# The 24 gate columns of w_in in a two-layer decoder trunk: two passes on packed high and low parts in place of three passes on a full tile

## The chip, the cores and the metric

One core of one Trainium2 chip runs the whole kernel. The metric is device time in microseconds of one execution, the median over several; the kernel before has 3276.86 us (three runs, 3276.48 to 3279.43).

## The reference, cut to what matters

The reference is a trunk of two layers on 1024 tokens of width 1024, all in float32. Each layer normalises and modulates x, and projects it with w_in. The projection is cut into pieces: three of 512 columns for a gated convolution, 512 for the queries, six of 128 for keys and values, **24 columns of gate logits** (three branches times eight heads), and 2048 for two merge gates:

```python
z = h @ w_in[l] + b_in[l]
(cb, cc, cu, q, kc, vc, k_s, v_s, k_w, v_w, nsa_g, merge_g) = jnp.split(z, split_at, axis=-1)
...
g = jax.nn.sigmoid(gate_logits).reshape(B, S, 3, N_KV, HPG)[..., None]
o = g[:, :, 0] * o_cmp + g[:, :, 1] * o_sel + g[:, :, 2] * o_w
```

The 24 logits of a token, after a sigmoid, weight the three attention branches (compressed, selected, windowed) of its eight heads. After attention come an up projection, a merge, an output projection, and a squared-ReLU MLP.

## The kernel before, in words

**Products with two parts.** A float32 product on TensorE is made of parts rounded to fp32r, a form that streams one column per clock. Activations lie as hH (high part) and hL (what is left), with features on partitions and 1024 tokens along the free axis. Each weight tile is 128 output columns wide and has eight blocks of 128 rows (k = 0 to 7). GpSimd (POOL) splits it: the high part goes to `unit` (L1158), the rest to `wlo` (L1160), in two halves of four blocks. `dense` (L1163 to L1189) then makes, for each k, three passes of two halves of 512 tokens: high weights with hH, high weights with hL, low weights with hH. That is 48 matmuls for a tile, all summed in one of the two PSUM slots `lin0` and `lin1`, which chunks take in turn. A tile is loaded by SyncE as soon as its place in a ring of five raw slots is free. POOL splits a tile once the matmuls that read the high part two tiles earlier are done.

**Order around the change.** The order is written out by hand on every engine. TensorE does q3, ks, kw, ns (the 24 gate columns), vw, then small work, then vs, then the attention loop. The tile "ns" is loaded and multiplied like any other, 128 columns wide, of which 24 are used. ScalarE, after its part of the rotary work for kw (L1668), waits for the chunk ns and takes rows 0 to 23 of it through a sigmoid with bias (L1702) into rows 0 to 23 of `tmp[:, 1, :]`, which frees the PSUM slot; then it evicts vw (L1644, through `z`). TensorE, after vw, turns those 24 rows to token-major with eight transposes (L1362) into `aux`, each 24 rows by 128 tokens. Then it makes the compressed scores of the last query tile (L1369, plain float32), turns vw to token-major into the same `aux` (L1277), waits for all rotary work (`rope_made`), makes the first score (L1403 to L1409), and multiplies vs. VectorE ends its rotary work with the low part of kw (L1964), copies the gates from `aux` to `gates` in `tmp` (L2011), which gives `aux` free for vw's turn, clears a small tile (L2019), and goes on with the compressed scores (L2028).

**What else sets the order.** vw's turn on TensorE waits for the semaphore `aux_free`; the first score waits for `rope_made` of all seven rotated pieces; the attention loop waits for chunk vs and ScalarE's eviction of it. POOL makes constant tables at the start (`begin_gpsimd`, L776 to L828), among them `ident`, and reports them by `tab_made`. Lines that the prediction's steps touch besides: L1344 and L1352 (second matmul of the compression, 64 and 63 columns of weights), L1292 (its first matmul), L1422 (transposes of 63 columns), L1443 and L1444 (values).

Of the kernel before, what the change touches and what calls it, by code (L numbers as in the profile page):

```python
# [48 lines left out]
O_KC, O_VC, O_KS, O_VS, O_KW, O_VW = (O_Q + NH * HD + i * NKV * HD for i in range(6))  # L49
O_NSA = O_VW + NKV * HD  # L50
NG = 3 * NH
O_MG = O_NSA + NG
IN_W = O_MG + 2 * D

# [269 lines left out]
def trunk(nc, a, out):  # L324

    with ExitStack() as ctx:
        def sb(name, shape, dt=F32):
            return ctx.enter_context(nc.sbuf_tensor(name, shape, dt))
# [57 lines left out]
        ident = sb("ident", [P, P])  # L386
        identb = sb("identb", [P, P], BF16)
        ones = sb("ones", [P, P])
        sgn = sb("sgn", [P, 1])
        causal = sb("causal", [P, P], BF16)  # L390
        oldest = sb("oldest", [P, P], BF16)
# [384 lines left out]
        def begin_gpsimd(pool):  # L776
            n = [0]

            def then(ins):
                n[0] += 1  # L780
                ins.then_inc(pool_step, 1)
                pool.wait_ge(pool_step, n[0])
# [15 lines left out]
                then(ins)  # L798
            pool.sem_inc(tab_made, 1)

            then(pool.memset(identb[:, :], 0.0))
            keep(identb[:, :], ALU.not_equal, [[-1, P]], 0, 1, 1.0)
            for i in range(4):
# [199 lines left out]
        def layer_programs(layer):  # L1003
# [18 lines left out]
            def freed(eng, name):  # L1022

                c = CHUNK[layer, name]
                eng.wait_ge(lin_free[c % 2], c // 2 + 1)
# [68 lines left out]
            def gpsimd(pool):  # L1094
                def attention():


                    for u in range(len(STEPS)):
                        for st in SETS:
                            for i in range(HPG):  # L1100
                                if st["last"] + SCALED_AFTER[i] == u:
# [2 lines left out]
                                    pool.tensor_scalar(p, p, fac[:, st["no"] % 2, i:i + 1], 1.0, ALU.mult, ALU.mult).then_inc(p_scaled, 1)  # L1104
                                    pool.wait_ge(p_scaled, HPG * st["no"] + i + 1)

                def pair_forms(n):


                    p = KIND_NO[n]  # L1110
                    a11, a12, a21, a22 = (raw_block(n, j, kh) for j in range(2) for kh in range(2))
                    s1, s2, s4, s3 = (form_part(unitF, n, i, 1) for i in (1, 3, 5, 6))

                    def form_sum(i, x, y, op):
                        if FORM_PRIOR[n][i]:
                            released(pool, FORM_PRIOR[n][i])
                        pool.tensor_tensor(form_part(unitF, n, i, 1), x, y, op).then_inc(w_sum, 1)  # L1117

                    def form_low(i, x):
                        pool.wait_ge(form_hi, PRODUCTS * p + i + 1)  # L1120
                        pool.tensor_tensor(form_part(unit, n, i, 1), x, form_part(unit, n, i, 0).bitcast(F32), ALU.subtract).then_inc(form_lo, 1)  # L1121

                    pool.wait_ge(raw_in[SLOT[n]], IN_SLOT[n])
                    form_sum(1, a21, a22, ALU.add)
                    form_low(0, a11)
                    pool.wait_ge(w_sum, 4 * p + 1)
                    form_sum(3, s1, a11, ALU.subtract)
                    pool.wait_ge(w_sum, 4 * p + 2)
                    form_low(1, s1)
                    form_low(2, a12)  # L1130
                    form_sum(5, a12, s2, ALU.subtract)
                    pool.wait_ge(w_sum, 4 * p + 3)
                    form_low(3, s2)
                    form_low(4, a22)
                    form_sum(6, a11, a21, ALU.subtract)
                    pool.wait_ge(w_sum, 4 * p + 4)
                    form_low(5, s4)
                    form_low(6, s3)

                for n in [m for m in WEIGHTS if TILES[m][1] == layer]:  # L1140
# [13 lines left out]
                    for i, hf in enumerate(half):  # L1154
                        raw, high = wraw[:, SLOT[n], hf], unit[:, HI_AT[n][i], :]
                        if HI_PRIOR[n][i]:
                            released(pool, HI_PRIOR[n][i])
                        pool.tensor_scalar(high, raw, 1.0, 1.0, ALU.mult, ALU.mult).then_inc(w_hi, 1)  # L1158
                        pool.wait_ge(w_hi, 2 * s + i + 1)
                        pool.tensor_tensor(wlo[:, SLOT[n], hf], raw, high.bitcast(F32), ALU.subtract).then_inc(w_split, 1)  # L1160

            def tensor(pe):
                def dense(name, act_h, act_l, ready=None, beside=None, only=None, midway=None):  # L1163
# [9 lines left out]
                    for k in range(kk):  # L1173
# [4 lines left out]
                        for c, n, s, r, j in parts:  # L1178
# [8 lines left out]
                                    mm = pe.matmul(lin[c % 2][:, hf], w, m(k, hf), start=first, stop=last)  # L1187
                            if k == kk - 1:
                                mm.then_inc(lin_done, 1)  # L1189

                def first_pair():

# [161 lines left out]
                mm.then_inc(cmp_done, 1)  # L1354
                dense("ks", H, L)
                dense("kw", H, L)
                dense("ns", H, L)
                dense("vw", H, L)
                aux_begin("nsaT")
                freed(pe, "ns")  # L1360
                for t in range(NT):
                    mm = pe.transpose(aux[:, t * NG:(t + 1) * NG], tmp[0:NG, 1, t * P:(t + 1) * P], ident[0:NG, 0:NG])  # L1362
                mm.then_inc(aux_done, 1)

                def compressed_scores(bank, qt):
# [207 lines left out]
            def scalar(act):  # L1573
# [112 lines left out]
                for r in range(2):  # L1686
# [12 lines left out]
                rope_high("kw")  # L1699
                done(act, "ns")  # L1700
                act.wait_ge(rope_made, ROPED.index("ks") + 1)
                act.activation(tmp[0:NG, 1, :], slot("ns")[0:NG, :], ACT.Sigmoid, bias=cols[0:NG, R_NSA:R_NSA + 1]  # L1702
                               ).then_inc(free_sem("ns"), 1)
                z("vw", B(O_VW))
                act.wait_ge(rope_sum, len(ROPED))
                v_high("vw", vw, aux[:, :])

# [174 lines left out]
            def vector(dve):  # L1882
# [124 lines left out]
                rope("q3")  # L2007
                rope("ks")
                rope("kw")
                dve.wait_ge(aux_done, AUXED.index("nsaT") + 1)  # L2010
                dve.tensor_copy(gates[:, :, :].rearrange("p t n -> p (t n)"), aux[:, 0:NT * NG]).then_inc(aux_free, 1)  # L2011
                dve.wait_ge(rope_made, len(ROPED))
                dve.wait_ge(aux_free, AUXED.index("nsaT") + 1)

# [374 lines left out]
```

## Time and profile before

| | us |
|---|---|
| median of three runs | 3276.86 |
| lowest, highest | 3276.48, 3279.43 |
| profiled execution, its own time | 3278.76 |
| its span, first to last instruction | 3277.0 |
| TensorE busy | 3171.2 (97% of the span) |
| VectorE busy | 1855.7 (57%) |
| GpSimd busy | 1544.1 (47%) |
| ScalarE busy | 972.1 (30%) |
| TensorE clock granted, mean | 0.988 of full |

The profiled execution took 1.8 us more than its span, and 1.9 us more than the median. Busy times of TensorE come from matmuls whose ends are modelled, so two neighbouring matmuls overlap in it; the distance of their starts is what one costs. The stage of the change comes once in each layer, near 514 to 539 us and near 2127 to 2152 us.

### The profile page before, as it was taken

Reading aid. Unit: us, or ns where it says so; the run is one execution under the profiler, and the core shown is the slowest. Engines: PE = TensorE matmul, PEld = TensorE weight load, DVE = VectorE, ACT = ScalarE, POOL = GpSimd, SP = SyncE. Lnnn points to the kernel's source line nnn. Section 1 sums busy time; section 2 is a strip of 40 time slices with the busy share of each in tenths; the row PEclk is TensorE's granted clock in tenths of the full one; section 3 lists DMA queues with packets and bytes.
Section 4 is the critical chain, followed back from the end, with each engine's and each line's share of the span. In section 5 each row is a group of like instructions: output and inputs, shape, how many; then the busy total and the mean of one; then the engine's idle time right before and its main releaser. Section 6 shows DMA issues by size and latency. Waiting matters only on the chain.

```text
span 3277.0 us, 40421 instructions
## 1 busy us (share of the span) xinstructions
PE 3171.2 (97%) x15183; PEld 2589.9 (79%) x15213; DVE 1855.7 (57%) x2507; ACT 972.1 (30%) x1771; POOL 1544.1 (47%) x1727
## 2 busy tenths in 40 slices
PE   8999999998899999999999999999989999999998
PEld 6888887676688888888778888877767888888887
DVE  7533246887536666555565332478864545555555
ACT  2100114666212222222220001257661222222233
POOL 3433332233454656666744333323334656666665
PEclk8999999999899999999999999999999999999999
DMA  7333621000522222111243345200005211111112
GB/s 262 119 116 129 187 77 39 1 1 1 199 62 68 78 78 78 52 52 52 78 144 99 119 141 174 59 20 1 1 14 199 65 52 52 52 52 52 52 52 97
DMA packets 294440, 264.16 MB, mean 81 GB/s; under 512 B 10347, under 2 KB 274791, under 8 KB 293736
## 3 DMA queue, kind: packets, MB, share of 16 engines
q1 hardware_dynamic: 279410, 207.66, 21.2%
q10 hardware_dynamic: 14838, 53.94, 4.4%
q8 instruction: 122, 2.00, 0.3%
q14 instruction: 70, 0.57, 0.1%
HBM read 223.81 MB, written 30.41 MB: 78 GB/s over the span
## 4 chain that ended last, share of the span: by engine, by line
PE 87%; DVE 8%; issue 2%; ACT 2%; POOL 1%; DMA 0%; ACTq 0%; DVEq 0%; POOLq 0%; SPq 0%
PE lin L1187 56%; PE lin L1536 16%; PE aux L1427 2%; DVE pTL L2119 2%; PE pv L1443 2%; PE pv L1444 1%; DVE negm L2095 1%; PE lin L1403 1%; PE lin L1404 1%; PE pv L1292 1%; ACT pTH L1754 1%; PE lin L1369 1%; PE lin L1237 1%; PE lin L1238 1%; PE lin L1239 1%
## 5 line engine op out<-in xcount | busy, mean ns | idle before, releaser
L1158 POOL TENSOR_SCALAR unit<-wraw 128x512 fp32r<-128x512 f32 x396 | 324.9, 820 | 1002.4 <-PE lin L1187 687.0
L1187 PE MATMUL lin<-hH,unit 128*128 128x512 f32 x2272 | 715.0, 391 | 1.2 <-POOL wlo L1160 1.2
L1187 PE MATMUL lin<-hL,unit 128*128 128x512 f32 x2272 | 710.9, 389 | 0.0
L1187 PE MATMUL lin<-hH,wlo 128*128 128x512 f32 x2272 | 710.4, 389 | 0.0
L1160 POOL TENSOR_TENSOR wlo<-wraw,unit 128x512 fp32r<-128x512 f32 x396 | 562.6, 1421 | 33.0
L1187 PEld LDWEIGHTS lin<-hH,wlo 128*128 128x128 f32 x2272 | 426.5, 188 | 89.8
L1187 PEld LDWEIGHTS lin<-hL,unit 128*128 128x128 f32 x2272 | 426.5, 188 | 89.1 <-issue 0.2
L1187 PEld LDWEIGHTS lin<-hH,unit 128*128 128x128 f32 x2272 | 423.4, 188 | 88.8 <-issue 2.8
L1536 PE MATMUL lin<-fH,unit 128*128 128x512 f32 x1568 | 486.8, 390 | 4.2 <-DVE xT L2255 3.5
L2255 DVE SCALAR_TENSOR_TENSOR xT<-lin,adac,xT 128x512 f32<-128x512 f32 x448 | 328.9, 748 | 182.5 <-PE lin L1536 177.8
L1104 POOL TENSOR_SCALAR prob<-prob,fac 128x640 f32<-128x640 f32 (+7 forms) x256 | 184.2, 719 | 441.6 <-DVE fac L2089 423.7
L1536 PEld LDWEIGHTS lin<-fH,unit 128*128 128x128 f32 x1568 | 294.4, 188 | 67.0 <-issue 6.1
L1536 PE MATMUL lin<-fL,unit 128*128 128x512 f32 x784 | 305.0, 389 | 0.0
L2119 DVE TENSOR_TENSOR pTL<-aux,pTH 128x512 fp32r<-128x512 f32 (+8 forms) x296 | 198.4, 686 | 60.9 <-ACT pTH L1754 59.1
L1754 ACT ACTIVATE pTH<-aux 128x512 fp32r<-128x512 f32 (+8 forms) x296 | 173.4, 596 | 110.5 <-PE aux L1427 82.0
L2199 DVE TENSOR_TENSOR stage<-stage 128x1024 f32<-128x1024 f32 x32 | 46.1, 1440 | 280.2 <-ACT stage L1825 280.2
L568 DVE SCALAR_TENSOR_TENSOR adared<-wraw,cT,adared 128x256 f32<-128x256 f32 x280 | 194.8, 696 | 13.5 <-DMA wraw<-in_w_ada 4.1
L2095 DVE TENSOR_REDUCE negm<-lin 128x1 f32<-128x640 f32 (+7 forms) x256 | 177.7, 703 | 41.8 <-PE lin L1409 40.8
L1723 ACT ACTIVATE prob<-lin,negm 128x640 f32<-128x640 f32 (+7 forms) x256 | 178.7, 698 | 70.7 <-DVE negm L2095 69.4
L1427 PE MATMUL aux<-ident,prob 128*128 128x128 f32 x1056 | 162.0, 280 | 35.4 <-DVE pTL L2119 33.9
L1121 POOL TENSOR_TENSOR unit<-unitF,unit 128x256 fp32r<-128x256 f32 x224 | 179.4, 812 | 13.2
L1841 ACT ACTIVATE unit<-unitF 128x256 fp32r<-128x256 f32 x224 | 93.6, 418 | 308.2 <-POOL unitF L1117 308.2
(282 smaller groups left out, 4461.5 us busy)
## 6 DMA issues: line engine op xcount, KB each, us to landing
wraw<-in_w_ff SPq DMA_DIRECT2D x136, 512.0 KB, 3.9
wraw<-in_w_ada SPq DMA_DIRECT2D x80, 512.0 KB, 3.7
wraw<-in_w_in SPq DMA_DIRECT2D x78, 512.0 KB, 4.9
wraw<-in_w_o SPq DMA_DIRECT2D x24, 512.0 KB, 3.9
adar<-in_w_ada SPq DMA_DIRECT2D x16, 512.0 KB, 11.8
x_keep<-xT ACTq DMA_DIRECT2D x4, 2048.0 KB, 8.6
mix_keep<-tmp ACTq DMA_DIRECT2D x16, 512.0 KB, 3.1
gate_keep<-ropes ACTq DMA_DIRECT2D x16, 512.0 KB, 6.7
```

The lines of the kernel that those rows point to most:

```text
L568: ins = dve.scalar_tensor_tensor(out=total, in0=w[:, i, :], scalar=c, in1=total, op0=ALU.mult, op1=ALU.add)
L1104: pool.tensor_scalar(p, p, fac[:, st["no"] % 2, i:i + 1], 1.0, ALU.mult, ALU.mult).then_inc(p_scaled, 1)
L1121: pool.tensor_tensor(form_part(unit, n, i, 1), x, form_part(unit, n, i, 0).bitcast(F32), ALU.subtract).then_inc(form_lo, 1)
L1158: pool.tensor_scalar(high, raw, 1.0, 1.0, ALU.mult, ALU.mult).then_inc(w_hi, 1)
L1160: pool.tensor_tensor(wlo[:, SLOT[n], hf], raw, high.bitcast(F32), ALU.subtract).then_inc(w_split, 1)
L1187: mm = pe.matmul(lin[c % 2][:, hf], w, m(k, hf), start=first, stop=last)
L1427: mm = pe.transpose(o[:, i * P:(i + 1) * P], prob_of(no, i)[:, x["at"]:x["at"] + P], ident[:, :])
L1536: mm = pe.matmul(bank, w[:, k, :], m[:, i, k, :], start=BEGINS[i] and w is wh and m is fH and k == 0, stop=w is wl and k == 1, skip_group_ ...
L1754: act.activation(pt("high", x, r), turned(x, r), ACT.Copy).then_inc(t_hi, 1)
L2095: dve.tensor_reduce(negm[:, m:m + 1], scores(u)[:, at:at + st["n"]], AX.X, ALU.max, negate=True).then_inc(max_made, 1)
L2119: dve.tensor_tensor(pt("low", x, r), turned(x, r), pt("high", x, r).bitcast(F32), ALU.subtract).then_inc(t_free[x["bank"]], 1)
L2255: dve.scalar_tensor_tensor(out=xT[:, i, half[h]], in0=home[HOME[q][role]], scalar=adac[:, 5 * KC + i:5 * KC + i + 1], in1=xT[:, i, half[h] ...
```

## The change

The tile ns is still loaded 128 columns wide. POOL now splits only its first columns, and puts both parts into the place of the high part: columns 0 to 31 of each block hold the high part of the tile's columns 0 to 31, columns 32 to 55 hold the low part of columns 0 to 23. TensorE makes two passes for each k: 56 columns of weights with hH, which gives high times hH in rows 0 to 23 of the slot and low times hH in rows 32 to 55; then 24 columns with hL, added to rows 0 to 23. ScalarE evicts 56 rows with the bias and no sigmoid. The turn to token-major becomes a matmul with `fold`, a constant of two identity blocks one above the other (rows 0 to 23 and 32 to 55), which turns and adds the two row groups at once. The sigmoid is then done by ScalarE from `aux` straight to `gates`, after the eviction of vw, and VectorE's copy is gone; so ScalarE now frees `aux`. `fold` is made by POOL at the start.

```diff
@@ constants, tables
+NG_LO = 32
+        fold = sb("fold", [P, NG])
+            then(pool.tensor_tensor(fold[:, :], ident[:, 0:NG], ident[:, NG_LO:NG_LO + NG], ALU.add))
@@ gpsimd
+                def narrow_split(raw, high, made):
+                    raw, high = (x.rearrange("p (k n) -> p k n", n=P) for x in (raw, high))
+                    pool.tensor_scalar(high[:, :, 0:NG_LO], raw[:, :, 0:NG_LO], 1.0, 1.0, ALU.mult, ALU.mult).then_inc(w_hi, 1)
+                    pool.wait_ge(w_hi, made)
+                    pool.tensor_tensor(high[:, :, NG_LO:NG_LO + NG], raw[:, :, 0:NG], high[:, :, 0:NG].bitcast(F32),
+                                       ALU.subtract).then_inc(w_split, 1)
...
+                        if t[6] == ["ns"]:
+                            narrow_split(raw, high, 2 * s + i + 1)
+                            continue
@@ tensor
+                def narrow(name, act_h, act_l):
+                    c, n = CHUNK[layer, name], TILE_OF[layer, name]
+                    s, out = KIND_NO[n], lin[c % 2]
+                    pe.wait_ge(lin_free[c % 2], c // 2)
+                    for k in range(KC):
+                        if k % (KC // 2) == 0:
+                            pe.wait_ge(w_split, 2 * s + 2 * k // KC + 1)
+                        for hf in half:
+                            pe.matmul(out[0:NG_LO + NG, hf], high_of(n, k * P, NG_LO + NG), act_h(k, hf), start=k == 0,
+                                      stop=False, skip_group_check=True)
+                        for hf in half:
+                            mm = pe.matmul(out[0:NG, hf], high_of(n, k * P, NG), act_l(k, hf), start=False,
+                                           stop=k == KC - 1, skip_group_check=True)
+                    mm.then_inc(lin_done, 1)
...
-                dense("ns", H, L)
+                narrow("ns", H, L)
                 dense("vw", H, L)
                 aux_begin("nsaT")
+                pe.wait_ge(tab_made, 3)
                 freed(pe, "ns")
                 for t in range(NT):
-                    mm = pe.transpose(aux[:, t * NG:(t + 1) * NG], tmp[0:NG, 1, t * P:(t + 1) * P], ident[0:NG, 0:NG])
+                    mm = pe.matmul(aux[:, t * NG:(t + 1) * NG], tmp[0:NG_LO + NG, 1, t * P:(t + 1) * P], fold[0:NG_LO + NG, :],
+                                   start=t == 0, stop=t == NT - 1, skip_group_check=True)
@@ scalar
-                act.activation(tmp[0:NG, 1, :], slot("ns")[0:NG, :], ACT.Sigmoid, bias=cols[0:NG, R_NSA:R_NSA + 1]
-                               ).then_inc(free_sem("ns"), 1)
+                act.activation(tmp[0:NG_LO + NG, 1, :], slot("ns")[0:NG_LO + NG, :], ACT.Identity,
+                               bias=cols[0:NG_LO + NG, R_NSA:R_NSA + 1]).then_inc(free_sem("ns"), 1)
                 z("vw", B(O_VW))
+                act.wait_ge(aux_done, AUXED.index("nsaT") + 1)
+                act.activation(gates[:, :, :].rearrange("p t n -> p (t n)"), aux[:, 0:NT * NG], ACT.Sigmoid).then_inc(aux_free, 1)
@@ vector
-                dve.wait_ge(aux_done, AUXED.index("nsaT") + 1)
-                dve.tensor_copy(gates[:, :, :].rearrange("p t n -> p (t n)"), aux[:, 0:NT * NG]).then_inc(aux_free, 1)
```

## Rows read from the trace of the kernel before

**Rows 1.** The page: busy times, and the chain that ended last, by engine and by line.
```profile
PE 3171.2 (97%) x15183; PEld 2589.9 (79%) x15213; DVE 1855.7 (57%) x2507; ACT 972.1 (30%) x1771; POOL 1544.1 (47%) x1727
PE 87%; DVE 8%; issue 2%; ACT 2%; POOL 1%; DMA 0%; ACTq 0%; DVEq 0%; POOLq 0%; SPq 0%
```

**Rows 2.** The chain, 490 to 560 us, in order: start, us, what.
```profile
491.84 43.74 PE lin L1187 x192
535.59 0.60 PE aux L1362 x8
```

**Rows 3.** Timeline of PE around ns, both layers: start, us, engine, line, op, names, count.
```profile
513.66 0.39 PE L1187 MATMUL lin<-hH,unit 128*128 128x512 f32 x1
524.54 0.39 PE L1187 MATMUL lin<-hH,unit 128*128 128x512 f32 x1
535.52 0.67 PE L1362 MATMUL aux<-ident,tmp 24*128 24x24 f32 x8
536.12 2.00 PE L1369 MATMUL pv<-kcmp,qS 128*128 128x63 f32 x16
538.75 0.42 PE L1403 MATMUL lin<-kwH,qS 128*128 128x384 f32 x1
...
2148.38 0.67 PE L1362 MATMUL aux<-ident,tmp 24*128 24x24 f32 x8
```

**Rows 4.** Timelines of PE and its weight loads, weights going 128, 64, 63, 128 columns.
```profile
470.32 0.61 PE L1187 MATMUL lin<-hH,wlo 128*128 128x512 f32 x2
470.87 0.41 PEld L1344 LDWEIGHTS pv<-tmp,w 128*64 128x64 f32 x4 [0.35 <-issue]
471.03 0.49 PE L1344 MATMUL pv<-tmp,w 128*64 128x126 f32 x3
...
491.39 0.45 PE L1352 MATMUL pv<-w,tmp 128*63 128x64 f32 x5
491.77 0.50 PE L1187 MATMUL lin<-hH,unit 128*128 128x512 f32 x1
492.11 0.39 PE L1187 MATMUL lin<-hH,unit 128*128 128x512 f32 x1
```

**Rows 5.** Timeline of PE where form or kind changes without a stop.
```profile
452.51 0.39 PE L1187 MATMUL lin<-hH,wlo 128*128 128x512 f32 x1
452.74 7.30 PE L1292 MATMUL pv<-blk,cmp_k 128*128 128x126 f32 x64
...
558.74 0.22 PE L1409 MATMUL lin<-causal,identb 128*128 128x128 bf16 x1
558.80 0.27 PE L1422 MATMUL aux<-ident,tmp 128*63 128x128 f32 x1
```

**Rows 6.** Timelines of ACT and DVE, 526 to 541 us.
```profile
531.17 1.11 ACT L1702 ACTIVATE tmp<-lin,cols 24x1024 f32<-24x1024 f32 x1
535.69 1.11 ACT L1644 ACTIVATE fbuf<-lin,cols 128x1024 f32<-128x1024 f32 x1 [3.41 <-PE lin L1187]
531.25 4.92 DVE L1964 TENSOR_TENSOR kwL<-ropes,kwH 64x1024 fp32r<-64x1024 f32 x4 [4.45 <-ACT kwH L1668]
536.22 0.36 DVE L2011 COPY tmp<-aux 128x192 f32<-128x192 f32 x1
538.22 0.68 DVE L2028 TENSOR_TENSOR scm<-pv,cmask 128x504 f32<-128x504 f32 x1 [1.38 <-PE pv L1369]
```

**Rows 7.** Timelines of ACT: small activations, 8 and 512 elements a partition.
```profile
6.65 0.18 ACT L892 ACTIVATE csig<-pv 128x8 f32<-128x8 f32 x1
559.44 0.59 ACT L1754 ACTIVATE pTH<-aux 63x512 fp32r<-63x512 f32 x1 [0.51 <-PE aux L1422]
```

**Rows 8.** Timeline of POOL: start of the kernel, split of ns.
```profile
33.62 0.62 POOL L1158 TENSOR_SCALAR unit<-wraw 128x512 fp32r<-128x512 f32 x1 [16.99 <-DMA wraw<-in_w_in]
503.13 0.62 POOL L1158 TENSOR_SCALAR unit<-wraw 128x512 fp32r<-128x512 f32 x1 [7.75 <-PE lin L1187]
503.84 1.29 POOL L1160 TENSOR_TENSOR wlo<-wraw,unit 128x512 fp32r<-128x512 f32 x1
```

## The prediction, made before the change was run

> **What bounds the kernel now.** I read the page first. TensorE is busy for 97% of the span, and of the chain that ended last 87% is TensorE [rows 1]. So a change in a dense stage is worth what it takes from TensorE's own queue there, unless another wait ends later. The chain through the stage confirms it: 192 matmuls of L1187 in a row, the tiles ks, kw, ns and vw, and the eight transposes of the gates right behind them, with nothing of another engine between [rows 2]. The timeline gives prices. The tile ns starts at 513.66 and vw at 524.54: 10.88 us for 48 matmuls, 0.227 us each; the transposes take 0.60 us, from 535.52 to 536.12 [rows 3]. The second layer's transposes start 1612.9 us later and are as long [rows 3], so I work out one layer and double it.
>
> **Matmuls removed.** Of 48, 16 go: 16 x 0.227 = 3.63 us per layer, all on the path. The 32 left still stream 512 tokens each, and I take 0.227 us for the streaming: 7.25 us.
>
> **What the new weight widths add.** This is where I differ from that simple count. In `dense` every matmul has 128 columns of weights and each load runs beside the matmul before. The new tile goes from 56 to 24 columns and back for every k. The trace has two places where ordinary products change from 128 columns to 64 or 63, and in both the load is not ahead. The last product of 512 columns starts at 470.55 (two of them, 0.22 apart, from 470.32), and the load for L1344 begins only at 470.87 [rows 4]: 0.32 us instead of 0.227, so 0.09 us for the stop. Then the load itself is exposed: the first L1344 takes 0.16 us to the second (470.87 to 471.03), the later ones 0.11, so 0.053 us for 64 columns [rows 4]. On the way back, the last L1352 starts at 491.62 (five from 491.39, 0.057 apart), L1187 follows 0.15 later, again 0.09 over, and the next L1187 comes after 0.34 in place of 0.227: 0.11 us for 128 columns [rows 4]. Where the width stays 128 there is no stop, although the product changes from fp32r to plain float32: L1292 starts 0.23 after the L1187 before it [rows 5]. So the change of form is what costs, not the type. By columns the exposed load is about 0.83 ns each (estimate from the 64 and the 128): 0.047 us for 56 and 0.020 us for 24.
>
> No row shows a change between two narrow widths. From below it costs 0, as in the transposes of 63 columns, which follow a bf16 matmul of 128 columns after 0.06 us, with no stop at all [rows 5]. From above I take 0.14 us a change, half again over the 0.09. I choose 0.09, because the products of L1344 and L1352 are the nearest in kind, and transposes are the only ones without a stop. Then ns costs 7.25 + 16 x 0.09 + 8 x (0.047 + 0.020) = 9.23 us, and the way back to vw adds 0.09 + 0.11 = 0.20. Together 9.43 against 10.88: **1.45 us gained per layer**, not 3.63.
>
> The rows alone give that choice. The Trainium skill (TensorEngine Tiling (Array Packing), section Key Properties) states a rule that speaks against this change: a change of tiling mode, not of the tile alone, drains the TensorE, and it lists 64 and 32 columns as different modes. The trace agrees for 128 to 64, with the 0.09 us; for 64 to 32 no row here shows it. By that rule ns would come to the 9.23 us, without it to 7.39 us and the sum to that of the first rival below.
>
> **The turn.** Eight transposes go and eight plain float32 matmuls come, with 128 columns of weights (tokens) and 24 moving. A plain float32 product shows as two instructions: the eight heads of the compressed scores are 16, from 536.12, the whole 2.00 us long with a last one of 0.28, so about 0.112 us each once they run, and 0.05 more for the first load [rows 3]. That is with 63 moving columns; the time is that of the weights, since 126 moving columns also give 0.112 (64 of L1292 in 7.30 us) [rows 5]. So 15 distances of 0.112, 0.05 for the first load, and 0.15 from the last to the next product, as behind L1352 [rows 4]: 1.88 us against 0.60. **1.28 us lost per layer.** From below the bound is 0.60, as the transposes had; from above 2.0.
>
> **ScalarE and VectorE.** The gate eviction stays 1.11 us and reads 56 rows in place of 24. It waits behind kw's rotary work, starts at 531.17 as before and ends at 532.28 [rows 6]. vw on TensorE would end about 535.5 - 1.45 = 534.1, so this is not a wait. vw's eviction moves to 534.3 to 535.4. Then the sigmoid of 128x192 waits for the turn, which ends near 536.1; by activations of 8 and of 512 elements it takes between 0.18 and 0.59 us [rows 7], I take 0.35, and `aux` is free at 536.5. On TensorE stand behind this wait vw's turn, and behind that the first score; but the compressed scores, 1.8 us, come first and end near 538.0, so it costs nothing. If that cover were gone it would cost 0.4. VectorE loses the copy of 0.36; its clearing waits for ScalarE until 536.5, but it has nothing to do before 537.9, when the scores are there (it idled 1.38 for them before) [rows 6]. The last rotary product ends at 536.17 and the first score starts at 538.75, so 2.5 us is the most that this stage could move up before kw is the wait [rows 3, 6].
>
> **POOL.** Two splits of 0.62 + 1.29 us become a quarter of the elements or less, some 3 us less per layer. POOL begins ns at 503.13, when ks frees the place, and TensorE wants it at 513.66; POOL stands still for 7 us before it [rows 8]. Worth nothing. vs's split waits for ns to end and comes 1.6 us earlier; it has 10 us before it is used. `fold` is one more operation of 128x24 at the start, some 0.3 us, before a wait of 17 us for the first weights [rows 8]. SyncE's and the other queues' DMAs stay as they are.
>
> **Sum.** -1.45 + 1.28 = -0.17 us per layer, -0.3 us for two. The profiled execution of 3278.8 would become 3278.5, and the median, which lies 1.9 below it, 3276.6. The measurement can tell about 0.2%, 6.6 us, from no change.
>
> **Rivals.** (1) *No stop between the two narrow widths.* Only the entry and the way back stop: ns takes 7.25 + 0.14, the way back 0.20, so 3.29 us less, then 1.28 lost in the turn; the gate eviction, ended at 532.28, then cuts off 0.2. 1.8 us per layer, 3.7 in all: 3273.2. For it speaks L1422. (2) *The turn is cheap as well*: another 1.3 us per layer, until kw's rotary work cuts it at 2.5 per layer: 3271.9. Against it stand all plain float32 products in the trace. This is also what a tile with unchanged widths would come near to, if the narrow forms were not treated as such. (3) *Slower: narrow fp32r products stream at half the rate.* No fp32r product with fewer than 128 columns of weights is in the trace. Its place is the 32 matmuls of ns, its price 32 x 0.227 = 7.25 us per layer, so 3276.6 + 14.5 = 3291.1. It decides once a narrow matmul costs 0.10 us more than I say. Against it: L1344 with 64 columns has 0.11 for 126 moving columns, as L1292 has with 128 [rows 4, 5].
>
> **How the numbers follow.** My forecast 0.62; no stop between narrow widths 0.25; both cheap 0.02; half rate 0.05; something unseen of a few us, either way, 0.06. Nothing that I can name reaches 6.6 us of gain: faster 0.03, for the unseen. Slower gets half rate and its share: 0.08. The rest, 0.89, is within 0.2%. The range holds the stops from 0 to 0.14 us (3273.2 to 3278.0), the turn's bounds, and the 3 us that runs of one kernel differ by: 3272.0 to 3280.0.
>
> **What would show it.** At the new line, pairs of narrow matmuls with distances of 0.27 and 0.32, then 0.25 and 0.32 us; each first weight load of a pair behind the matmul before, put down to "issue". ns start to vw start 9.3 us (7.4 by the first rival, 16.5 by half rate). The turn: 16 instructions in 1.9 us. The compressed scores start near 536.1, and the first score near 538.6. The forecast is wrong if the score starts before 537.5 or after 540, or if TensorE waits for `aux`.

## The result, and the profile after

The changed kernel takes **3288.48 us** (median of 8, 3286.59 to 3289.87) against 3278.46 for the kernel before on the same chips (8 runs, 3276.27 to 3280.67): ratio 1.0028, 95% interval 1.0018 to 1.0038. It is slower, by some 10 us, where I had forecast 0.3 us less and a range that ended at 3280.0. Its profiled execution took 3289.87 us, 1.4 above its median, with a span of 3288.0.

The page of the changed kernel, busy times and the chain by engine; they answer to [rows 1]:

```profile
PE 3174.7 (97%) x15167; PEld 2588.8 (79%) x15197; DVE 1860.8 (57%) x2505; ACT 971.0 (30%) x1773; POOL 1539.1 (47%) x1728
PE 86%; DVE 9%; ACT 3%; issue 2%; POOL 0%; DMA 0%; ACTq 0%; DVEq 0%; POOLq 0%; SPq 0%
```

TensorE's share of the chain fell by one point, those of VectorE and ScalarE rose by one each: somewhere the end now hangs on them. And TensorE is busy 3.5 us longer although it has 16 fewer matmul instructions: some of them became slower.

The narrow tile itself isn't at fault. Timeline of TensorE in the changed kernel, from the last dense product before ns to the first after it:

```profile
515.43 0.61 PE L1202 MATMUL lin<-hH,wlo 128*128 128x512 f32 x2
515.89 0.63 PE L1216 MATMUL lin<-hH,unit 128*56 128x512 f32 x2
516.36 0.62 PE L1219 MATMUL lin<-hL,unit 128*24 128x512 f32 x2
...
522.86 0.63 PE L1219 MATMUL lin<-hL,unit 128*24 128x512 f32 x2
523.33 0.62 PE L1202 MATMUL lin<-hH,unit 128*128 128x512 f32 x2
```

The pairs start 0.46 or 0.47 apart, dense pairs 0.45: 32 products in 523.33 - 515.89 = 7.44 us, 0.232 each. So there is no stop on the way in, between 56 and 24 columns, or on the way out. The tile took 10.88 us before [rows 3].

The loss lies behind it. The chain of the changed kernel through this stage, in order of time (start, us, what):

```profile
525.48 2.13 DVE ropes L1979
527.61 1.56 DVE ropes L1982
...
529.19 2.21 DVE ropes L1987
...
535.75 1.12 ACT tmp L1736
...
537.00 3.58 PE aux L1395 x16
540.58 3.60 PE pv L1403 x16
544.18 1.71 PE aux L1309 x8
```

Before, this chain was TensorE's alone [rows 2]. Now it runs through kw's three rotary operations on VectorE, the copies of kw on ScalarE (left out here), ScalarE's eviction of the gates (L1736), and only then the turn. TensorE's own row for the turn names the wait, and the products behind it are twice as long as before:

```profile
537.00 3.58 PE L1395 MATMUL aux<-fold,tmp 56*128 56x24 f32 x16 [2.62 <-ACT tmp L1736]
540.51 3.67 PE L1403 MATMUL pv<-kcmp,qS 128*128 128x63 f32 x16
543.97 1.92 PE L1309 MATMUL aux<-ident,fbuf 128*128 128x128 f32 x8
545.54 0.67 PE L1437 MATMUL lin<-kwH,qS 128*128 128x384 f32 x1
...
2154.25 3.30 PE L1395 MATMUL aux<-fold,tmp 56*128 56x24 f32 x16 [2.62 <-ACT tmp L1736]
```

The compressed scores took 2.00 us before [rows 3] and take 3.67; the first products of the first score 0.42 and 0.67. Windows over the same stretch give the reason (window, us, then busy time and number of PE, PEld, DVE, ACT and POOL, then the granted clock, DMA share and GB/s):

```profile
515.90:523.30 7.40, 7.40 (x33) 3.72 (x32) 3.90 (x3) 4.41 (x5) 3.80 (x4) 1.00 0.23 52
534.00:537.00 3.00, 0.38 (x2) 0.03 (x1) 1.17 (x1) 2.95 (x4) 0.00 (x0) 0.94 0.48 141
537.00:540.50 3.50, 3.50 (x16) 3.45 (x16) 3.46 (x4) 0.86 (x1) 0.00 (x0) 0.50 0.08 29
540.50:544.00 3.50, 3.50 (x18) 3.50 (x18) 0.35 (x2) 0.33 (x1) 0.00 (x0) 0.50 0.00 0
544.00:547.00 3.00, 3.00 (x16) 2.65 (x15) 2.04 (x3) 1.02 (x1) 0.00 (x0) 0.52 0.00 0
547.00:550.00 3.00, 3.00 (x15) 2.49 (x15) 2.89 (x5) 1.92 (x3) 0.00 (x0) 1.00 0.00 0
```

The narrow tile ran at a granted clock of 1.00 (2.4 GHz). TensorE then stood still for 2.62 us, and the clock was 0.50 (1.2 GHz) for the ten microseconds of small products behind that. It had fallen shortly before the turn began (0.94 in the window 534 to 537). The second layer is alike, only that there it fell 0.3 us behind the start of the turn, whose first two distances are still 0.11 us and the later ones 0.21.

Why ScalarE is late is seen on POOL and VectorE. POOL of the changed kernel, the four operations for vs:

```profile
523.68 0.62 POOL L1173 TENSOR_SCALAR unit<-wraw 128x512 fp32r<-128x512 f32 x1 [3.48 <-PE lin L1219]
524.39 2.13 POOL L1175 TENSOR_TENSOR wlo<-wraw,unit 128x512 fp32r<-128x512 f32 x1
526.50 1.59 POOL L1173 TENSOR_SCALAR unit<-wraw 128x512 fp32r<-128x512 f32 x1
528.17 2.14 POOL L1175 TENSOR_TENSOR wlo<-wraw,unit 128x512 fp32r<-128x512 f32 x1
```

and VectorE beside it:

```profile
525.48 2.13 DVE L1979 TENSOR_TENSOR ropes<-fbuf,cosT 128x1024 f32<-128x1024 f32 x1
527.53 1.62 DVE L1982 TENSOR_TENSOR ropes<-rotated,sinT 128x1024 f32<-128x1024 f32 x1
529.19 2.20 DVE L1987 TENSOR_TENSOR ropes<-ropes 128x1024 f32<-128x1024 f32 x1
```

In the kernel before these three operations were:

```profile
522.88 1.23 DVE L1943 TENSOR_TENSOR ropes<-fbuf,cosT 128x1024 f32<-128x1024 f32 x1
524.02 1.22 DVE L1946 TENSOR_TENSOR ropes<-rotated,sinT 128x1024 f32<-128x1024 f32 x1
525.28 1.52 DVE L1951 TENSOR_TENSOR ropes<-ropes 128x1024 f32<-128x1024 f32 x1
```

and POOL's split of vs was:

```profile
524.89 0.83 POOL L1158 TENSOR_SCALAR unit<-wraw 128x512 fp32r<-128x512 f32 x1 [6.90 <-PE lin L1187]
525.80 2.14 POOL L1160 TENSOR_TENSOR wlo<-wraw,unit 128x512 fp32r<-128x512 f32 x1
...
528.62 1.29 POOL L1160 TENSOR_TENSOR wlo<-wraw,unit 128x512 fp32r<-128x512 f32 x1
```

POOL may start vs's split when ns is done on TensorE. Counted from the first instruction of the tile ks (491.77 before, 494.00 in the changed kernel), that now happens 3.4 us earlier, at 29.7 in place of 33.1. VectorE's work for kw does not move with it (31.5, before 31.1): the two that used to overlap for about one operation now overlap throughout. Both lose: VectorE's operations take 1.62 to 2.20 us, POOL's subtractions 2.13 and 2.14 and its second copy 1.59, where undisturbed ones take 1.29 and 0.62.

The stage can be laid out in microseconds from the start of the tile ks, layer 0 / layer 1. These are starts of the first instruction of each group, and the end of the last kwL operation; the last column is the first product of the next group of scores, behind the tile vs:

| kernel | ScalarE's gate eviction | kwL ends | turn | scores | vw's turn | first score | next score group |
|---|---|---|---|---|---|---|---|
| before | 39.40 / 39.38 | 44.39 / 44.38 | 43.75 / 43.75 | 44.35 / 44.35 | 46.18 / 46.18 | 46.98 / 46.98 | 60.30 / 60.30 |
| after | 41.75 / 41.75 | 46.75 / 46.75 | 43.01 / 43.01 | 46.51 / 46.24 | 49.98 / 49.70 | 51.54 / 51.27 | 65.47 / 65.62 |

So per layer: without the wait the turn would start at 40.32 (seen below), 3.43 us before the old 43.75. The wait takes back 2.69 (2.62 by its row, where the end before it is modelled); the turn costs 3.50 in place of 0.60, the scores 3.47 in place of 1.83, vw's turn 1.56 in place of 0.80, and the stretch up to the next score group 13.93 in place of 13.32: together 5.2 us lost in layer 0 and 5.3 in layer 1, 10.5 of the 11.0 by which the spans differ. The rest is made of pieces of both signs elsewhere (+2.2 us before the first tile ks, -2.5 and -1.1 in the two attention loops, +1.7 between the layers, +0.2 at the end), which also differ among the kernels below.

Much of the difference in the loops is the clock again. From the next score group to the last score of the loop the changed kernel takes 283.3 us in layer 0, with a granted clock of 0.50 for 2.4 us of it; the kernel before takes 285.7, with 10.2 us at 0.50, in its profiled execution. Among the profiled executions of all kernels here the loop takes 281.8 to 282.2 us in layer 0 with none of it at 0.50, 282.8 to 283.4 with 3.4 us at 0.50, and 284.7 with 6.8.

### The profile page after: what moved, and what is told of

It reads as the page before. It is cut to its first block, busy times and chain, and to the rows that moved or that the text cites. A ratio compares the mean times of both kernels' runs of the same rounds, so it can differ in the third digit from the quotient of the medians.

```text
span 3288.0 us, 40392 instructions
## 1 busy us (share of the span) xinstructions
PE 3174.7 (97%) x15167; PEld 2588.8 (79%) x15197; DVE 1860.8 (57%) x2505; ACT 971.0 (30%) x1773; POOL 1539.1 (47%) x1728
## 4 chain that ended last, share of the span: by engine, by line
PE 86%; DVE 9%; ACT 3%; issue 2%; POOL 0%; DMA 0%; ACTq 0%; DVEq 0%; POOLq 0%; SPq 0%
PE lin L1202 54%; PE lin L1570 16%; PE aux L1461 2%; DVE pTL L2153 2%; PE pv L1477 2%; PE pv L1478 1%; PE lin L1437 1%; DVE negm L2129 1%; PE lin L1438 1%; PE pv L1324 1%; ACT pTH L1790 1%; PE lin L1403 1%; PE lin L1269 1%; PE lin L1270 1%; PE lin L1271 1%
## 5 line engine op out<-in xcount | busy, mean ns | idle before, releaser
L1202 PE MATMUL lin<-hH,unit 128*128 128x512 f32 x2240 | 706.6, 392 | 1.5 <-POOL wlo L1175 1.5
L1202 PE MATMUL lin<-hL,unit 128*128 128x512 f32 x2240 | 701.5, 390 | 0.0
L1202 PE MATMUL lin<-hH,wlo 128*128 128x512 f32 x2240 | 700.9, 389 | 0.0
```

## The experiments

My theory after seeing this: POOL's earlier split slows kw's rotary work, the gate eviction, queued behind kw's copies on ScalarE, comes late, and TensorE's wait lets the clock fall. The rivals: the narrow tile or the plain products of the turn themselves bring the clock down, or the turn is the cost whatever else is done. Each experiment has runs of the kernel before beside it, with medians from 3277.81 to 3279.77, and the ratios are to these. The changed kernel was measured beside 3278.46, so a distance from it can be off by some 1.3 us. The layout of the stage, in the same measure, each row from one profiled execution (e7 has that of the kernel before within 0.01):

| kernel | gate eviction | kwL ends | turn | scores | vw's turn | first score | next score group |
|---|---|---|---|---|---|---|---|
| e1_evict_first | 31.48 / 31.48 | 46.75 / 46.75 | 40.32 / 40.32 | 42.21 / 42.21 | 45.30 / 44.04 | 46.86 / 46.81 | 61.38 / 60.14 |
| e2_split_late | 39.08 / 39.08 | 44.08 / 44.08 | 40.33 / 40.34 | 42.21 / 42.21 | 44.04 / 44.81 | 44.85 / 46.38 | 58.14 / 59.80 |
| e3_both | 31.09 / 31.09 | 44.08 / 44.08 | 40.32 / 40.32 | 42.21 / 42.21 | 44.04 / 44.04 | 44.84 / 44.84 | 58.14 / 58.16 |
| e4_full_width | 39.37 / 39.37 | 44.36 / 44.37 | 43.75 / 43.75 | 45.64 / 45.64 | 47.47 / 48.27 | 48.27 / 49.83 | 61.57 / 64.81 |
| e5_add_before_turn | 31.10 / 31.09 | 44.02 / 44.02 | 40.32 / 40.32 | 40.92 / 40.92 | 42.75 / 42.76 | 44.07 / 44.07 | 57.38 / 57.40 |
| e8_scores_first | 41.76 / 41.76 | 46.75 / 46.75 | 43.01 / 43.01 | 40.23 / 40.23 | 45.36 / 46.51 | 46.98 / 48.13 | 61.08 / 62.47 |
| e9_pool_beside | 41.68 / 41.66 | 46.67 / 46.66 | 43.75 / 43.75 | 44.35 / 44.35 | 47.12 / 47.10 | 47.97 / 47.95 | 61.29 / 61.26 |
| e10_gates_late | 39.37 / 39.37 | 44.37 / 44.37 | 46.23 / 46.23 | 46.83 / 47.20 | 48.66 / 50.67 | 50.19 / 52.24 | 64.40 / 66.05 |

(In e10 the eviction named is the first of six; the one that counts starts 5.7 us later.)

**Eviction of the gates ahead of kw's copies** (on the changed kernel):

```diff
@@ scalar
-                rope_high("kw")
                 done(act, "ns")
                 act.wait_ge(rope_made, ROPED.index("ks") + 1)
                 act.activation(tmp[0:NG_LO + NG, 1, :], slot("ns")[0:NG_LO + NG, :], ACT.Identity, ...)
+                rope_high("kw")
```

> The changed kernel with one thing moved: ScalarE evicts the gate chunk before kw's rotary copies and not behind them. Queue theory (TensorE waits for the gate eviction, which stands behind kw's copies; the idle stretch of 2.8 us makes the clock fall to half, and turn, scores and vw's turn take double): the turn starts right behind vw, the granted clock stays 1.00, the turn takes 1.9 us, and the first score then waits for the end of kw's rotary work, so it comes 4.7 us earlier per layer: about 3279. Rival (the narrow products or the new turn lower the clock themselves): the turn still runs at half clock and takes 3.3 us or more, at best 2.8 us per layer are gained: 3283 or more.

Measured: 3282.78 us, ratio to before 1.0011 (1.0001 to 1.0020), 5.7 below the changed kernel. The turn starts at 40.32 without a wait. kw still ends at 46.75, and now the first score waits for it in layer 1, at 46.81. In layer 0 the clock fell even without a wait ahead of the turn: scores 3.1 us in place of 1.8. So the wait is a real cost, and it isn't the only thing that brings the clock down; neither of my two forecasts (3279, or 3283 and more) describes both layers.

**POOL splits vs only after all rotary work** (on the changed kernel):

```diff
@@ gpsimd, ahead of a tile's split
+                    if t[6] == ["vs"]:
+                        pool.wait_ge(rope_sum, len(ROPED))
```

> The changed kernel with one wait added: POOL splits vs only when VectorE has made the rotary sum of kw, so that it does not share the time with VectorE's rotary work. If the earlier split is what makes kw late: VectorE's four operations before it take 1.2 to 1.5 us each again, kw's copies start 2.3 us earlier, TensorE waits under 0.5 us, the clock stays full, the first score comes 6.2 us earlier per layer: about 3276. If kw is late for another reason, or the clock falls for another reason: 3286 to 3289, as without it.

Measured: 3276.1 us, 0.9996 (0.9987 to 1.0005), 12 below the changed kernel: its whole loss. VectorE is back at its old durations:

```profile
522.78 1.23 DVE L1981 TENSOR_TENSOR ropes<-fbuf,cosT 128x1024 f32<-128x1024 f32 x1
...
525.17 1.22 DVE L1989 TENSOR_TENSOR ropes<-ropes 128x1024 f32<-128x1024 f32 x1
```

kw ends at 44.08 in place of 46.75, the eviction starts at 39.08, and the turn waits for nothing. In layer 1 the clock still fell once, during the scores. This is the experiment that puts the cause on POOL's timing, two lines of code that leave TensorE's and ScalarE's programs as they are.

**Both** (the two edits together):

> Both edits, the eviction first and the late split of vs. Queue theory: no wait on TensorE between ks and the first score, turn 1.9 us at full clock, first score 2.0 us earlier than in the kernel before, 4 us in all: 3274.5. Rival (clock falls by the narrow products or the turn): 3283 or more.

Measured: 3278.27 us, 0.9996 (0.9987 to 1.0005). In the profiled execution the stage is free of clock falls in both layers, and the first score comes at 44.84, 2.1 us per layer before the old one. The median, 3278.27 against 3279.03 and with an interval that holds 1, shows none of those 4.3 us clearly; its runs lie between 3272.8 and 3283.6. The mean granted clock goes with it: 0.990 in the three fastest executions, 0.986 in the slowest. So the slow end has more time at 0.50. Whether that lies in this stage, as in one layer each of e1 and e2, or in the attention loops isn't shown, since only one execution was profiled (3275.36 us).

**Gates 128 columns wide, new turn kept** (on the changed kernel; its turn adds rows of other columns to the gates):

```diff
-                narrow("ns", H, L)
+                dense("ns", H, L)
@@ gpsimd
-                        if t[6] == ["ns"]:
+                        if False:
```

> The changed kernel with the gate tile again split and multiplied over its full 128 columns in three passes; the turn by the sum matrix and the late sigmoid stay (it then adds rows of other columns to the gates, so the output is another). Queue theory: vw ends as late as before, the eviction is done by then, the clock stays full, and the stage is longer by the turn alone, 1.3 us per layer: 3281. If the new turn itself brought the clock down: 3287. So this prices the turn by itself.

Measured: 3285.15 us, 1.0019 (1.0009 to 1.0028). I had said 3281. The price of the turn alone is seen in layer 0: at full clock the scores start 45.64 - 44.35 = 1.29 us later than before. In layer 1 the clock fell to 0.50 during the scores, and the next score group came 4.5 us later than before. There was no narrow product, and no wait ahead of the turn.

**Add before the turn, on VectorE** (e3 with this edit):

```diff
@@ scalar, ahead of kw's copies
-                act.activation(tmp[0:NG_LO + NG, 1, :], slot("ns")[0:NG_LO + NG, :], ACT.Identity, ...)
+                act.activation(tmp[0:NG, 1, :], slot("ns")[NG_LO:NG_LO + NG, :], ACT.Copy).then_inc(blk_made, 1)
@@ vector, after kw's rotary sum
+                    if name == "kw":
+                        dve.wait_ge(blk_made, 3)
+                        dve.scalar_tensor_tensor(out=tmp[0:NG, 1, :], in0=slot("ns")[0:NG, :], scalar=cols[0:NG, R_NSA:R_NSA + 1],
+                                                 in1=tmp[0:NG, 1, :], op0=ALU.add, op1=ALU.add).then_inc(free_sem("ns"), 1)
@@ tensor
-                    mm = pe.matmul(aux[...], tmp[0:NG_LO + NG, 1, ...], fold[0:NG_LO + NG, :], ...)
+                    mm = pe.transpose(aux[...], tmp[0:NG, 1, ...], ident[0:NG, 0:NG])
```

> The narrow tile and both changes of order of the third experiment are kept (ScalarE takes the chunk ns ahead of kw's rotary copies, POOL splits vs only after all rotary work), and the turn by a product with fold is taken out: ScalarE copies rows 32 to 55 of the slot to rows 0 to 23 of tmp, VectorE adds rows 0 to 23 and the bias to them in the time in which it waits for kw, and the turn is the eight transposes again. If the turn's form is the rest of the cost, its eight transposes take 0.60 us in place of 1.88, and the first score of a layer starts at about 44.2 us after the start of tile ks (before: 46.98), since kw's rotary work, done at 44.1, is then the wait: 2.8 us less per layer than the kernel before, some 3273.4 us in all if the granted clock stays full (before: 3279.0 in the runs so far). If the one small operation that VectorE now has ahead of its last pieces makes kw late, the score starts later by as much as it lasts (0.5 to 1 us). If something else than the turn and the collision costs time, the stage stays at 44.8 or more.

Measured: **3271.49 us** (7 runs, 3269.80 to 3274.33) against 3279.77: 0.9974 (0.9963 to 0.9985), faster than both kernels. Its timeline (VectorE's new operation, then TensorE):

```profile
527.19 1.27 DVE L1991 SCALAR_TENSOR_TENSOR tmp<-lin,cols,tmp 24x1024 f32<-24x1024 f32 x1
531.53 4.92 DVE L2004 TENSOR_TENSOR kwL<-ropes,kwH 64x1024 fp32r<-64x1024 f32 x4 [3.07 <-ACT kwH L1703]
...
533.35 2.00 PE L1404 MATMUL pv<-kcmp,qS 128*128 128x63 f32 x16
...
536.50 0.44 PE L1438 MATMUL lin<-kwH,qS 128*128 128x384 f32 x1 [0.27 <-DVE kwL L2004]
```

VectorE's 1.27 us lie in the time in which it waits for ScalarE, still 3.07 long. The first score starts 0.05 us after kw is ready, 2.9 us per layer before the old one: kw's rotary work is now the bound of this stage. The stages give 5.8 of the 8.3 us. The profiled execution shows 3.7 more in layer 0's attention loop (294.8 us from the next score group to its end, before 298.5), where no part of the edit is. The clock goes with it: up to the last score of the loop 281.9 us with none of it at 0.50, before 285.7 with 10.2 us at 0.50. Why the clock falls there in one execution and not in another isn't shown, so I count only the 5.8 us as the edit's.

**The compression's second product 128 columns wide** (on the kernel before), for the stop at L1344:

```diff
-                    mm = pe.matmul(pv[0:HD, 0, 256:256 + 2 * NC], w2[:, 0, hc, :], hsil[:, hc, :], ...)
+                    mm = pe.matmul(pv[:, 0, 256:256 + 2 * NC], w2[...][:, HD * hc:HD * hc + P], hsil[:, hc, :], ...)
```

> The kernel before, with one edit: the weights of the compression's second product are taken 128 columns wide in place of 64 (the further rows that this gives are not read by anyone). In the kernel before the first of these loads was not ahead of its product: 0.32 us from the last dense product in place of 0.227. If it was the width in plain float32 that stopped the engine, the distance falls to about 0.23 us and the load runs beside the dense product. If the plain float32 form or the wait for data stopped it, it stays at 0.32 us. The time of the whole kernel does not change by anything that can be measured (0.1 us at most per product group).

Measured: one run, 3277.62 us, no difference that one run can show. Its TensorE and weight loads:

```profile
470.94 0.62 PE L1187 MATMUL lin<-hH,wlo 128*128 128x512 f32 x2
471.39 0.60 PE L1344 MATMUL pv<-tmp,w 128*128 128x126 f32 x4
...
471.17 0.64 PEld L1344 LDWEIGHTS pv<-tmp,w 128*128 128x128 f32 x4
```

The second of the two dense products starts at about 471.16, L1344 at 471.39: 0.23 us, and its load starts at 471.17, beside that product. With 64 columns it came 0.32 us after the last dense one began, behind it [rows 4]. So it was the width, in a plain float32 product; a like step, from 128 to 56, costs nothing in the fp32r products of ns.

**Scores ahead of the turn** (on the changed kernel; the block of L1390 to L1397 moved behind the compressed scores):

> The changed kernel, with the turn of the gates moved behind the compressed scores on TensorE, so that TensorE has work while ScalarE's eviction of the gates is late. If it is the wait of 2.6 us ahead of the turn that lets the granted clock fall to 0.50, the clock stays at 1.00 here: scores from 40.3 to 42.2 us after the start of tile ks, a wait of about 0.7 us for the eviction (it ends at 41.75, the scores at 42.2, so perhaps none), the turn until 44.1, vw's turn until 45.9, and the first score at 46.8 since kw's rotary work ends at 46.75: 4.5 us less per layer than the changed kernel, 3279 to 3280 us. If the small products of turn, scores and vw's turn bring the clock down whatever stands ahead of them, they run at half of it here too (turn 3.5 us in place of 1.9), and the score starts at 50 or later, 3285 us or more.

Measured: 3281.06 us, 1.0001 (0.9991 to 1.0010), 7.4 below the changed kernel. My number for the eviction was its start, not its end (42.86), so there still was a wait, of 0.9 us in place of 2.7:

```profile
535.43 1.93 PE L1481 MATMUL aux<-fold,tmp 56*128 56x24 f32 x16 [0.89 <-ACT tmp L1736]
537.78 1.97 PE L1309 MATMUL aux<-ident,fbuf 128*128 128x128 f32 x8 [0.42 <-ACT tmp L1740]
```

The second wait, 0.42 us for the sigmoid, is what the prediction had priced at 0.4 for the case that the scores don't cover it. The clock stayed at 1.00 through the turn of layer 0 (1.93 us) and fell behind it; in layer 1 it fell in the turn. So the result lies between the two theories: less standing still, later and shorter at 0.50, but not none.

**POOL busy beside kw's rotary work** (on the kernel before; four more operations, of no use):

```diff
@@ gpsimd, ahead of vs's split
+                    if t[6] == ["vs"]:
+                        pool.wait_ge(z_made, Z.index("kw") + 1)
+                        for i in range(4):
+                            raw = wraw[:, SLOT[n], half[i % 2]]
+                            pool.tensor_scalar(raw, raw, 1.0, 1.0, ALU.mult, ALU.mult).then_inc(pool_step, 1)
+                            ...
```

> The kernel before (gates 128 columns wide, nothing narrow), with four more operations of 128x512 on POOL, started when VectorE begins kw's rotary work and of no use (they multiply the raw tile vs by 1). If POOL's work beside VectorE's rotary work is what makes that work slow in the changed kernel, the three rotary operations of kw take 1.6 to 2.2 us each here as well (before: 1.2 to 1.5), kw's low part ends at 46 to 47 us after the start of tile ks in place of 44.4, and ScalarE's eviction of the gates ends at 41 or later in place of 39.4. TensorE needs the eviction at 43.7 and kw at 47.0, so the time should hardly change (0 to 1 us per layer). If the narrow tile slowed them in some other way, the three stay at 1.2 to 1.5 us.

Measured: 3277.96 us, 0.9995 (0.9986 to 1.0004). POOL's four and VectorE's three:

```profile
518.79 5.41 POOL L1160 TENSOR_SCALAR wraw<-wraw 128x512 f32<-128x512 f32 x4 [0.83 <-ACT fbuf L1652]
...
523.81 1.46 DVE L1951 TENSOR_TENSOR ropes<-fbuf,cosT 128x1024 f32<-128x1024 f32 x1
525.19 1.63 DVE L1954 TENSOR_TENSOR ropes<-rotated,sinT 128x1024 f32<-128x1024 f32 x1
526.85 2.19 DVE L1959 TENSOR_TENSOR ropes<-ropes 128x1024 f32<-128x1024 f32 x1
```

Without anything narrow VectorE's second and third operations take as long as in the changed kernel (1.63 and 2.19), and kw ends at 46.67, 2.3 us late. The four useless operations didn't stand where I wanted them: they ran from 518.79 to 524.20, for the most part beside VectorE's low part of ks (L1972), which takes 6.15 us in place of 5.18. So kw's rotary work began 1.0 us later (32.07 in place of 31.11 in the measure of the tables) and met vs's own split, which stands where it always did (33.09). Both are POOL's work beside VectorE's. The delay costs TensorE only 1.0 us per layer in the stage (vw's turn waits for VectorE's copy of the gates), since it asks for the gates at 43.75 and the eviction ended at 42.8. So the same delay does little harm with a tile of 10.88 us and is decisive with one of 7.44.

**Gates late by ScalarE alone** (on the kernel before; the sigmoid eviction made five times more ahead of the one that counts):

> The kernel before (gates 128 columns wide, turn by transposes), with ScalarE's eviction of the gates made five times before the one that counts: each is 1.11 us, so it ends some 5.5 us later, about 46.1 us after the start of tile ks, and TensorE waits some 2.3 us for it (turn at 46.1 in place of 43.75). This is the wait of the changed kernel without its narrow products and without its plain products in the turn. If the wait is enough to bring the granted clock down, it is 0.50 behind the turn in both layers here too, scores and vw's turn take twice as long, and the first score comes at 52 or later, 5 us or more per layer over the kernel before. If it takes the longer row of plain float32 products (turn, scores and vw's turn, 5.6 us in one piece) as well, the clock stays at 1.00, and the first score comes at about 49.3, 2.3 us per layer over the kernel before, 4.6 us in all.

Measured: 3288.70 us, 1.0031 (1.0020 to 1.0041), which is the time of the changed kernel. TensorE, both layers:

```profile
540.28 0.67 PE L1362 MATMUL aux<-ident,tmp 24*128 24x24 f32 x8 [2.41 <-ACT tmp L1706]
540.88 2.00 PE L1369 MATMUL pv<-kcmp,qS 128*128 128x63 f32 x16
542.71 1.88 PE L1277 MATMUL aux<-ident,fbuf 128*128 128x128 f32 x8
...
2154.19 1.05 PE L1362 MATMUL aux<-ident,tmp 24*128 24x24 f32 x8 [2.41 <-ACT tmp L1706]
2155.17 3.67 PE L1369 MATMUL pv<-kcmp,qS 128*128 128x63 f32 x16
```

Wide tile, old turn, and a wait of 2.41 us: the clock fell to 0.50 in both layers. In layer 1 it fell within the wait (0.95 over its 2.4 us, 0.50 over the transposes), in layer 0 at vw's turn, 2.5 us after TensorE had resumed. I had said a first score at 52 or later in both layers; it is 52.24 in layer 1 and 50.19 in layer 0, where the scores still ran at full clock. By the next score group the two layers are 4.1 and 5.8 us behind the kernel before, 9.9 of the 10.4 by which the spans differ.

**Together.** In the profiled executions, one of each kernel, layers in which the clock fell within the stage: all 6 of those with a wait of 0.9 us or more ahead of the turn (after, e8, e10); 3 of 8 with the long turn and no wait ahead of it (e1, e2, e3, e4); none of 8 with the short turn and no such wait (before, e5, e7, e9). With a wait of 2.4 us or more the fall is there in every layer; the long turn without a wait makes it possible. What decides it from one layer to the next in the middle group stays open.

## Why the prediction was wrong, point by point

*Matmuls removed.* 16 x 0.227 = 3.63 us: right as a count. The turn could start 3.43 us earlier, the difference being the 0.005 us by which each of the 32 narrow products is slower.

*What the new weight widths add.* I had 9.43 us for ns and the way back; it was 7.44, with 0.01 for the way back. Every part was wrong: the stops (0.09 each), the exposed loads, the stop on the way in. I had concluded from L1344 that "the change of form is what costs, not the type". Row L1292 had only shown that type alone costs nothing; that width costs something only together with the type is what e7 and the narrow tile show. The 0.25 case of my first rival was the right one, and its 7.39 us close. Its 1.8 us gained per layer is near the 2.2 that e3 shows in its profiled execution, once nothing collides and the clock stays up. The Trainium skill (TensorEngine Tiling (Array Packing), section Key Properties) says that a change of tiling mode drains the engine; between 128, 56 and 24 columns of fp32r weights the rows show distances of 0.23 us and no drain. So either this change of width is no change of mode, or it drains nothing that these rows show; no run here tells which.

*The turn.* 1.28 us lost per layer predicted, 1.29 measured in e4 at full clock. Right, and by the step that I had named: with 24 moving columns the instructions of the turn start 0.112 us apart there, as those of the scores do with 63. In the changed kernel itself the turn took 3.50 us, for the clock.

*ScalarE and VectorE.* "It waits behind kw's rotary work, starts at 531.17 as before": that sentence named the right place and kept the wrong number. Against the 40.32 of the turn even the old start was no full cover: 39.40 + 1.11 = 40.51, the 0.2 us that only my first rival had. With the start at 41.75 it became a wait of 2.69 us. The rest held: the sigmoid took 0.33 us for the 0.35 I took, and costs the named 0.4 when the scores don't cover it (e8).

*POOL: the step that failed.* "vs's split waits for ns to end and comes 1.6 us earlier; it has 10 us before it is used": it had no term in the sum. I had asked only who waits for the split, not what runs beside it. The trace of before already had the collision, in a place where it did little harm: kw's last rotary sum is 1.52 us where the others are 1.22 and 1.23, and the vs subtraction beside it 2.14 us where the next is 1.29. The split came 3.4 us earlier, not 1.6, since the tile became shorter than I had said. Its four operations, 3.8 us when undisturbed, then cost VectorE 2.4 us on the way to the eviction, which started at 41.75 in place of 39.40. Held back in e2, the split cost nothing.

A rule for it stands in the Trainium skill (SBUF — State Buffer, section Who interferes with whom): a VectorE instruction with two SBUF inputs and a GpSimd instruction that reads SBUF want the same read port, and the second waits for the first. All three rotary operations have two such inputs. The traces agree in direction, on both engines, with 1.2 going to 2.2 and 1.3 to 2.1 us; they don't show the port itself.

*The clock: the second step that failed.* The sum had no term for it at all; every small product behind the turn was priced at full clock. Of the 5.2 us lost in the stage of layer 0, it is the largest part: at full clock the turn from 43.01 on would take 1.89, the scores 1.83 and vw's turn 0.80, which puts the first score at 47.53, not 51.54. So the change with its late eviction would have cost 0.55 us per layer (47.53 - 46.98); the clock behind it costs 4.0, and 0.6 more by the next score group.

*The rivals.* My slower case had 3291.1, near the 3288.5 measured, for a reason that did not hold (narrow products at half the rate). A time that comes near doesn't confirm a mechanism: its own sign, ns of 16.5 us, was absent. The line on what would prove me wrong did name the right signs: the score started at 545.5 where 540 was the limit (543.3 without the 2.2 us by which this execution was late at the tile ks). I had only thought of a wait for `aux`, not for the eviction.

## What to carry to other kernels

When a tile gets shorter, ask for every engine that its end releases what it will now run beside, not only who waits for the result; a cover is gone as soon as the work in front of it is shorter, so compare end times anew for each step moved. A wait on TensorE in front of a stretch of small products is to be priced with those products at 1.2 GHz: here a wait of 2.4 us in each of two layers cost 10.9 us in all (e10). And two passes on packed parts do pay here (8.3 us, 0.26%, by the medians of e5, of which its stages show 5.8), once the adding is done by an idle VectorE, POOL's split is held back until the rotary work is done, and the eviction is not queued behind it.

## What the runs showed of the hardware that I had not expected

- fp32r products with 56 and with 24 columns of weights follow each other and 128-column ones at 0.23 us for 512 moving columns, loads ahead. A like step to 64 columns in plain float32 stops the engine for 0.09 us, and widening it to 128 takes the stop away (e7).
- POOL's copy of 128x512 goes from 0.62 to 1.59 us and its subtraction from 1.29 to 2.14 beside VectorE's operations on two operands, which go from 1.22 to 2.20.
- With a wait of 2.41 us the granted clock was 0.50 in both layers (e10): in one it fell before TensorE resumed, in the other 2.5 us after. Small products without a wait ahead of the turn had it in 3 layers of 8 where the turn was the long one.
- The attention loop of layer 0 takes 281.8 us with none of it at 0.50 (e10) and 285.7 with 10.2 us at 0.50 (before), with the same work in it. A median can hold several microseconds of this that no edit made.
